# Retention by chunks with a carried state, and token-row jobs 512 columns wide in quarters of the depth

## The reference

```python
def retention_branch(p, cos, sin):            # S = 512, 4 heads, q and k 64 wide, v 128 wide
    q, k, v, g = jnp.split(p, ...)
    q = rotary(q, cos, sin); k = rotary(k, cos, sin) * (RET_QK_DIM ** -0.5)
    # chunks of 128 tokens, a decay gamma_h for each head
    scores = jnp.einsum('bhnid,bhnjd->bhnij', qc, kc) * decay_in[:, None]   # inside a chunk, j <= i
    inner = jnp.einsum('bhnij,bhnje->bhnie', scores, vc)
    kv = jnp.einsum('bhnjd,bhnje,hj->nbhde', kc, vc, k_dec)                 # what a chunk adds to the state
    R = R * chunk_decay + kv_n                                              # carried over the chunks
    cross = jnp.einsum('bhnid,nbhde,hi->bhnie', qc, R_prev, q_dec)
    y = inner + cross
    y = y * lax.rsqrt(jnp.mean(y * y, axis=-1, keepdims=True) + EPS)
    return y * jax.nn.silu(g)
```

## Time and profile before

| | |
|---|---|
| three runs | 2812.18, 2813.51, 2815.59 us; median 2813.51 |
| profiled execution | span 2810.8 us, 46630 instructions; the page gives no time of its own beside the span |
| TensorE | busy 2760.1 us, 98%, 18980 records |
| VectorE, ScalarE, GpSimd | 46%, 39%, 50% |
| granted TensorE clock | mean 0.997 |
| DMA | 413.98 MB, mean 147 GB/s |
| first stage, layer one | jobs 4 to 17: 41.95 to 143.67 us |
| first stage, layer two | jobs 4 to 17: 956.52 to 1059.04 us |

### The profile page before, as it was taken

How to read it: one execution, slowest core, us unless ns; L and a number is a source line. 1 busy time by engine, 2 the same in 40 slices (tenths; PEclk the granted TensorE clock), 3 DMA queues, 4 the chain that set the end, 5 groups by cost and what they waited for, 6 DMA issues and landing times. The chain is left out here.

```text
span 2810.8 us, 46630 instructions
## 1 busy us (share of the span) xinstructions
PE 2760.1 (98%) x18980; PEld 2059.2 (73%) x18981; DVE 1286.0 (46%) x1791; ACT 1101.1 (39%) x1618; POOL 1399.4 (50%) x1767
## 2 busy tenths in 40 slices
PE   8999999999999999999999999999999999999997
PEld 6777778888888877777788888877778764445543
DVE  6255433467751524543446775168855232222223
ACT  5485334343332448533434333355574321111112
POOL 6377446666665637744666665665655321111110
PEclk9999999999999999999999999999999999999999
DMA  5222122222232422212222223232222149999995
GB/s 182 74 87 73 48 106 91 85 93 103 91 112 98 163 75 87 72 49 105 91 86 91 105 90 113 93 113 81 93 91 94 63 190 407 419 415 411 414 409 232
DMA packets 63368, 413.98 MB, mean 147 GB/s; under 512 B 9792, under 2 KB 10560, under 8 KB 25920
## 3 DMA queue, kind: packets, MB, share of 16 engines
q1 hardware_dynamic: 63168, 411.18, 38.6%
HBM read 401.71 MB, written 4.19 MB: 144 GB/s over the span
## 5 line engine op out<-in xcount | busy, mean ns | idle before, releaser
L113 POOL TENSOR_TENSOR w_lo<-w,next_hi 128x256 fp32r<-128x256 f32 (+1 forms) x1272 | 1001.5, 820 | 623.4 <-ACT next_hi L1686 290.1
L1686 ACT CAST next_hi<-w 128x1024 fp32r<-128x1024 f32 (+1 forms) x152 | 156.9, 1032 | 462.4 <-PE bank L1504 443.0
L113 POOL TENSOR_TENSOR mid_w_lo<-w,mid_w_hi 128x256 fp32r<-128x256 f32 x240 | 198.6, 859 | 138.8 <-ACT mid_w_hi L2812 138.4
L3574 PE MATMUL bank<-moe_w,moe_hg 128*64 128x512 f32 x1024 | 225.8, 594 | 0.0
L3574 PEld LDWEIGHTS bank<-moe_w,moe_hg 128*64 128x64 f32 x1024 | 73.4, 137 | 141.1 <-issue 141.1
L3511 POOL COPY moe_quad_place<-moe_place 128x16 f32 (+1 forms) x7 | 1.4, 196 | 346.5 <-PE bank L3628 346.5
L1499 PE MATMUL bank<-h_hi,next_hi 128*128 128x512 f32 x688 | 170.8, 390 | 0.0
L1504 PE MATMUL bank<-h_hi,w_lo 128*128 128x512 f32 x688 | 169.9, 389 | 0.0
L1501 PE MATMUL bank<-h_lo,next_hi 128*128 128x512 f32 x688 | 169.9, 389 | 0.0
L1332 ACT CAST next_hi<-w 128x1024 fp32r<-128x1024 f32 x96 | 80.2, 835 | 206.6 <-PE bank L1530 151.6
L1499 PEld LDWEIGHTS bank<-h_hi,next_hi 128*128 128x128 f32 x688 | 129.1, 188 | 27.7 <-issue 1.0
(11 more groups left out here) (633 smaller groups left out, 6243.3 us busy)
## 6 DMA issues: line engine op xcount, KB each, us to landing
moe_w<-in_moe_w SPq DMA_DIRECT2D x128, 1024.0 KB, 13.1
moe_w<-in_moe_w SPq DMA_DIRECT2D x32, 2048.0 KB, 12.4
w<-in_ffn_up SPq DMA_DIRECT2D x44, 1024.0 KB, 4.8
w<-in_w_merge SPq DMA_DIRECT2D x48, 768.0 KB, 4.3
w<-in_w_in SPq DMA_DIRECT2D x30, 1024.0 KB, 4.8
w<-in_w_mid SPq DMA_DIRECT2D x29, 1024.0 KB, 4.8
w<-in_ffn_down SPq DMA_DIRECT2D x16, 1408.0 KB, 5.8
w<-in_w_out SPq DMA_DIRECT2D x16, 512.0 KB, 4.3
```

What stands on the lines that cost most here:

```text
L113: ins = nc.gpsimd.tensor_tensor(out[:, ks, :], raw[:, ks, :], high[:, ks, :].bitcast(F32), ALU.subtract)
L1686: nc.scalar.copy(split(B.w_hi, n), raw(n)).then_inc(f["w_hi"], 1)
L3574: mm = nc.tensor.matmul(bank[half_of(u), :], hg[:, k, slots_of(b, u)], w[:, u, k * 512:k * 512 + 512], start=(k == 0), stop=(k == KD - 1))
```

## The change

Retention follows the reference's chunks. The decay table holds 128 columns a head instead of 512, and a new table `qdec` (2 x 128 columns) holds the decay of the queries. VectorE multiplies the queries of chunks 1 to 3 with it (`decay_queries`). Behind job 8 TensorE transposes the keys of chunks 0 to 2 (`turn_keys`, 6 transposes into banks 6 and 7) and makes the scores inside the chunks of all four heads (`scores`, 16 matmuls of 64 rows and 128 columns, alternating between the two row halves, banks 2 to 5). VectorE writes the keys with their decay (`take_keys`) and the decayed scores (`decays`, one operation a head). Behind job 9 come the states that the chunks add (`chunk_states`, 12 matmuls of 128 rows with 64 columns stationary, alternating between the column halves); VectorE carries them on (`states`). Behind jobs 10 and 11 `values(t)` adds for two heads the products inside the chunks (8 matmuls of 128x128) and with the states (6 of 64 rows, alternating), into bank 2 + h. `squares` comes behind jobs 11 to 14; on ScalarE `square` in jobs 10 to 13 and `root` in jobs 11 to 14, root ahead of square.

A pair of token chunks is 512 columns in four quarters of the depth. A token job is a quarter: 4 token tiles x 3 products x 2 steps = 24 matmuls of 512 columns, a bank for each token tile, in the order 2, 3, 0, 1. ScalarE takes the tiles in the fourth quarter, three while it runs and one after it. The weights are laid out for it outside of the kernel. The first quarter of jobs 14 to 17 waits for `ret_done` of 2, as banks 2 and 3 are those of heads 0 and 1.

```diff
-        self.vt, self.decay = at(spare, 0, "vt", 4, S), at(y_rw, 0, "decay", RET_HEADS, S)
+        self.vt, self.decay = at(spare, 0, "vt", 4, S), at(y_rw, 0, "decay", RET_HEADS, P)
+        self.ktok, self.kv = at(y_rw, 2, "ktok", 2, 3, P), at(y_rw, 5, "kv", 2, 3, P)
+        self.qdec, self.qd = at(bonus, 4, "qdec", 2, P), at(spare, 8, "qd", 2, S)
...
+            sync.dma_start(B.qdec[:, :, :], T.dram["ret_qdec"]).then_inc(f["ret_loaded"], 16)
...
-                for m in range(4):
-                    bank = T.ps[m // 2][:, (m % 2) * 256:(m % 2) * 256 + 256]
-                    if t == 0 and m % 2 == 0:
-                        pe.wait_ge(f["took"][m // 2], c)
+                if quarter == 0 and i >= 2:
+                    pe.wait_ge(f["ret_done"], 2)
+                for m in TOKEN_TILES:
+                    if quarter == 0 and m < 2:
+                        pe.wait_ge(f["took"][m], c)
                     for lhs, w in ((h_hi, hi), (h_lo, hi), (h_hi, lo)):
-                        for k in range(half):
-                            if w is lo and m == 0:
-                                pe.wait_ge(f["w_lo"], pieces_until(n, k, half))
+                        for k in range(2):
+                            if w is lo and m == TOKEN_TILES[0]:
+                                pe.wait_ge(f["w_lo"], pieces_until(n, 2 * k + 1, half))
+                            mm = nc.tensor.matmul(T.ps[m][:, :], lhs(2 * quarter + k)[:, m * P:m * P + P], w[:, k, :], ...)
...
+            def scores():
+                pe.wait_ge(f["rotated"], 4)
+                for t in range(2):
+                    for c in range(4):
+                        now = slice(c * P, c * P + P)
+                        for u in range(2):
+                            q = slice(64 * u, 64 * u + 64)
+                            mm = nc.tensor.matmul(T.ps[2 + 2 * t + u][:, now], qk[q, 2 + t, now], qk[q, t, now],
+                                                  start=True, stop=True)
+                    mm.then_inc(f["ret_products"], 1)
+            def turn_keys():
+                        mm = nc.tensor.transpose(T.ps[6 + t][:, c * P:c * P + P], qk[:, 2 + t, c * P:c * P + P],
+                                                 T.ident[:, :])
+            def chunk_states():
+                            mm = nc.tensor.matmul(T.ps[6 + t][64 * u:64 * u + 64, c * P:c * P + P],
+                                                  B.ktok[:, t, c, 64 * u:64 * u + 64], vt[:, c, h * P:h * P + P],
+                                                  start=True, stop=True)
+            def values(t):
+                pe.wait_ge(f["ret_decayed"], SCORES_DECAYED + 2 * t + 2)
+                for c in range(4):
+                    for u in range(2):
+                        nc.tensor.matmul(T.ps[2 + h][:, c * P:c * P + P], vt[:, c, h * P:h * P + P],
+                                         B.sc[:, h, c * P:c * P + P], start=(c == 0), stop=False, ...)
+                pe.wait_ge(f["kv_ready"], t + 1)
+                for c in range(1, 4):
+                    for u in range(2):
+                        mm = nc.tensor.matmul(T.ps[2 + 2 * t + u][:, c * P:c * P + P], B.kv[q, t, c - 1, :],
+                                              B.qd[q, t, c * P:c * P + P], start=False, stop=(c == 3), ...)
...
-                if n in (10, 12, 14, 16):
-                    squares((n - 10) // 2)
-                if n in (8, 10, 12, 14):
-                    scores((n - 8) // 2)
-                if n in (9, 11, 13, 15):
-                    values((n - 9) // 2)
+                if n == 8:
+                    turn_keys()
+                    scores()
+                if n == 9:
+                    chunk_states()
+                if n in (10, 11):
+                    values(n - 10)
+                if n in (11, 12, 13, 14):
+                    squares(n - 11)
...
-                if n in (9, 11, 13, 15):
-                    square((n - 9) // 2)
-                if n in (10, 12, 14, 16):
-                    root((n - 10) // 2)
+                if n in (11, 12, 13, 14):
+                    root(n - 11)
+                if n in (10, 11, 12, 13):
+                    square(n - 10)
...
+            def states(t):
+                dve.wait_ge(f["ret_products"], STATES_SUMMED + t + 1)
+                link(nc.vector.tensor_copy(B.kv[:, t, 0, :], T.ps[6 + t][:, 0:P]))
+                for c in range(1, 3):
+                    ins = nc.vector.scalar_tensor_tensor(out=B.kv[:, t, c, :], in0=B.kv[:, t, c - 1, :],
+                                                         scalar=B.qdec[:, t, P - 1:P],
+                                                         in1=T.ps[6 + t][:, c * P:c * P + P], op0=ALU.mult, op1=ALU.add)
```

More of the change, by code:

```diff
@@ L225 @@
 TOKEN_CHUNKS = (2, 3, 7, 8)
+TOKEN_TILES = (2, 3, 0, 1)
 RW_FIRST, U_FIRST = 18, 30
@@ L413, in feature_job @@
                 mm.then_inc(f["done"], 1)
-            def scores(h):
-                q = slice(64 * (h % 2), 64 * (h % 2) + 64)
+            def scores():
                 pe.wait_ge(f["rotated"], 4)
-                for jc in range(4):
-                    if h:
-                        pe.wait_ge(f["decayed"], 4 * (h - 1) + jc + 1)
-                    nc.tensor.matmul(T.ps[2 + jc][:, 0:S - jc * P], qk[q, 2 + h // 2, jc * P:jc * P + P],
-                                     qk[q, h // 2, jc * P:S], start=True, stop=True).then_inc(f["scored"], 1)
@@ L425, in values @@
-            def values(h):
-                if h == 0:
-                    for t in range(2):
-                        pe.wait_ge(f["took"][t], 4)
-                else:
-                    pe.wait_ge(f["ret_done"], h)
-                for jc in range(4):
-                    pe.wait_ge(f["decayed"], 4 * h + jc + 1)
-                    mm = nc.tensor.matmul(T.ps[6][:, jc * P:S], vt[:, jc, h * P:h * P + P],
-                                          B.sc[:, jc, 0:S - jc * P], start=(jc == 0), stop=(jc == 3),
-                                          skip_group_check=True)
-                mm.then_inc(f["summed"], 1)
+                for t in range(2):
[6 more added lines that the diff above has]
+                    mm.then_inc(f["ret_products"], 1)
@@ L861, in _ @@
                 rotate(t)
+            dve.wait_ge(f["rotated"], 4)
+            for t in range(2):
+                decay_queries(t)
+            for t in range(2):
+                take_keys(t)
             for h in range(RET_HEADS):
                 decays(h)
-                if h == 3:
-                    shift(12, 12, B.sg_tmp[:, 0, :])
-                    shift(13, 13, B.sg_tmp[:, 1, :])
+            for t in range(2):
+                states(t)
+            for h in range(RET_HEADS):
+                if h >= 2:
+                    shift(10 + h, 10 + h, B.sg_tmp[:, h - 2, :])
                 head_out(h)
@@ L3999, in layout @@
     w_in = weight_chunks(np.concatenate([a["w_in"][:, :, cols], a["w_in"][:, :, len(cols):]], axis=-1), 256)
+    for n in range(0, len(TOKEN_CHUNKS), 2):
+        both = [FRONT_ORDER[c] for c in TOKEN_CHUNKS[n:n + 2]]
+        columns = w_in[:, both].reshape(L, 2, P, 2, KD // 2, 256)
+        w_in[:, both] = columns.transpose(0, 3, 2, 4, 1, 5).reshape(L, 2, P, -1)
     out["w_in"] = w_in[:, :FRONT_CHUNKS]
```

116 lines of the change are left out of this document (77 added, 39 removed).

## The result

The changed kernel took 2791.61 us (median of 4 runs, 2789.2 to 2796.58), the kernel before 2813.78 (2812.18 to 2815.59) beside it: ratio 0.9924, 95% interval 0.9909 to 0.9938. The forecast was 2790.0. Five more runs later gave 2798.84 (2789.96 to 2799.42), ratio 0.9939, interval 0.9926 to 0.9953. All nine together have a median of 2792.4, but they lie in two heaps, five at 2789.2 to 2792.4 and four at 2796.6 to 2799.4, while the kernel before, run beside them, kept to 2811.7 to 2816.5 (over all its 39 runs on record, 38 lie at 2811.7 to 2817.4 and one at 2821.5). So there are two questions: whether the 23.5 us of the sum are there, and what takes back some 7 us in some executions.

A forecast was written before the change was run, and what follows sets the result against it. TensorE, busy 98% of the span, was taken as the bound. Terms 5.1 + 17.4 + 1.1 - 0.5 + 0.45 = 23.5 us, taken from 2813.5, gave 2790.0 us (chance 0.73), range 2785.5 to 2800.

The forecast's parts named there:

- Token jobs: 16 token jobs over two layers: 24 matmuls of 512 columns take 5.44 us a job instead of 5.76; 5.1 us gained.
- Retention: TensorE's work behind jobs 8 to 11: 9.9 us a layer instead of 18.6, matmuls pairing on two halves; 17.4 us gained.
- Job 18: TensorE's 0.55 us wait for a tile of `v` at the start of job 18 goes; 1.1 us gained for two layers.
- ScalarE's loop: Root and square in each of jobs 11 to 14: 6.3 us against TensorE's 6.4, 0.1 to spare; 0.5 us charged.
- Low half at job 6: Cast and POOL's four pieces for a pair's first quarter: 5.7 us against 6.6, so hidden, 0.9 to spare.
- Weight of job 6 in layer two: 640 KB less ahead of it in the queue, landing 1.6 to 1.9 us sooner, wait about 0.1; 0.45 us gained.
- Stages: The two stages, one in each layer, were to be shorter by some 11.6 and 12 us, all else as before.
- The stages behind move forward as a block.: Stages after the changed ones start by TensorE's progress and TensorE is full there too, so the whole gain reaches the span.
- rival 4: Stage ends earlier but the last stage's expert-weight streaming takes the time back; no change, 2812 us; chance 0.03.
- rival 1: Retention matmuls on the two halves don't pair at 128 columns, costing 8.9 us; 2798.9 us; chance 0.12.

The follow-up runs named there:

- tokens_narrow: Changed kernel with each 512-column matmul of the token jobs made as two of 256 columns; 2799.69 us.
- one_half: Changed kernel with scores, cross products and chunk states of both heads on the same array half, so nothing can pair (output wrong); 2804.47 us.
- tables_late: Changed kernel with masks, centre and mixing tables fetched behind the weights of chunks 3 and 4 instead of ahead of them; 2796.54 us.
- late_and_shift: Changed kernel with masks, centre and mixing tables fetched behind later weights, plus 64 extra satisfied waits on TensorE in layer two; 2788.5 us.
- changed_again: The changed kernel itself, unedited, in five more runs; 2798.84 us, the profiled execution 2789.96 us.
- rows_in_turn: Changed kernel with scores and cross products made all on one row half, then all on the other, instead of alternating; 2798.54 us.
- square_twice: Changed kernel with ScalarE computing each of the four squares a second time into an unread tile; 2797.74 us (two runs).
- tables_heavy: Changed kernel with two tables loaded a second time at the head of the stage, 640 KB more, read by nobody; 2795.87 us (two runs).
- cols_in_turn: Changed kernel with the chunk states made all on one column half, then all on the other, instead of alternating; 2797.55 us.

## Why the prediction was right, and where it wasn't

- **Token jobs, 5.1 us.** Jobs 4 to 7 measure 22.03 us, less 0.15 of a wait at job 6 (the 0.77 at 53.40 us where others are 0.62): 5.47 a job for 5.44. tokens_narrow gives 4.4 us for both layers. Right.
- **Retention, 17.4 us.** Behind jobs 8 to 11 stand 2.75, 1.7, 2.9 and 2.9 us, 10.3 for 9.9, so 16.7 us gained for 17.4. The mechanism, pairs on two halves, is shown by one_half (8.7 us). The size was off by 6 ns a record: 62 and not 56, and by the going in and out, 0.4 us for 0.3. The 81 ns at 128 columns that was quoted from the Trainium skill ("TensorE: Matmul & The Clock Gate", Back-to-back issue gap) is no floor for records on alternating halves.
- **Job 18, 1.1 us.** Gone in both layers.
- **ScalarE's loop, -0.5 us.** It idles 0.4 to 0.5 us a round, 0.1 had been reckoned, and TensorE never waits for it. The 0.5 us that was charged for nothing makes up most of the 0.7 by which retention fell short: the sum came out close partly by luck. Job 14 starts at 109.27 us and its token tile's release (VectorE's second head) ends at 109.12: 0.15 to spare for the 0.2 predicted.
- **Low half at job 6, "0.9 to spare".** Wrong. In layer one the fourth piece is 0.15 us late even with the cast on time; POOL's pieces are slower there than half of its eight.
- **Weight of job 6 in layer two, 0.45 us.** That fewer bytes ahead bring it forward is shown by tables_late and late_and_shift. The size was too good: the cast came 1.2 us sooner against job 4 (8.20 to 7.02), for 1.6 to 1.9, and the wait stayed at 0.6 us in this execution, and was nil in changed_again (cast at 6.51). With the same bytes three edited kernels had it at 8.6 to 10.1 and waited 1.76 us, more than the 1.65 that the prediction had for a weight that comes no sooner. So in the profiles the term runs from a gain of 0.5 us to a loss of 1.2 and the reduced clock behind it.
- **Stages.** 11.2 and 11.3 us shorter in the first profile, 11.2 and 12.0 in changed_again, for 11.6 and 12.
- **"The stages behind move forward as a block."** That held in the two profiled executions to within 1.2 us, and by their times in five of nine. The other four are some 7 us longer (2796.6 to 2799.4 for 2789.2 to 2792.4). The likeliest value was right; the mean of the nine, 2794.3, lies 4 us above it. What fails, at least in the kernels with one edit more, is the assumption that outside the stage only data and engines can be late. The refill of TensorE's own instructions is a transfer too, and the edits moved it against the merge transfers. No rival named it; rival 4 had asked for a transfer that doesn't start by TensorE's progress, and this one does, but by the count of its instructions. Whether the changed kernel's four long executions have this stall, the late weight of job 6 or the reduced clock of the last stage wasn't seen, since the two that were profiled took 2791.25 and 2789.96 us. Why the kernel before doesn't spread so (in its one profile the recurrence has no such gap above 0.6 us) is argued from where its refills fall, not tried.
- **What the time alone would have said.** The later five runs have a median of 2798.84 us, which is the 2798.9 of rival 1, though the halves do pair. Only the rows of the stage tell the two apart.

## What to carry to other kernels

Put small matmuls of two heads on the two halves of the array in alternation, and keep them together: each going in and out costs as much as six of their records. If a kernel that got shorter spreads over two values, look in the trace for a gap of the bounding engine with no releaser, and then at the instruction queue under it. Look also at the wait for a weight behind a full queue, which differed by 1.8 us between profiles here. A few harmless instructions, or a large transfer moved, can be worth more than the next edit.

## What the runs showed of the hardware

- Records of 128 columns: 111 ns alone, 115 to 117 when all are on one half, 62 in alternation. A sequence of one half overlaps with the sequence of the other half behind it (rows_in_turn: 86 ns a record on average).
- TensorE's instructions come in packets of 16 KB, on average one for 267 records (matmuls and weight loads). That they are TensorE's is read from their coming at nearly the same record numbers of it in each execution. One that fell behind a transfer of 768 KB waited for its end, and TensorE started again 2.4 us after that packet's start (1236.77 to 1239.14). In tables_late it ran dry 178 records behind the place of the undisturbed refill. The Trainium skill ("Runtime: NRT & Kernel Launch", Instruction fetch mechanics) has the cost of crossing such a block mostly hidden; the measurement decides otherwise where a large transfer is ahead of it.
- Behind such a gap the granted clock was 0.50, 1.2 GHz, for 6.8 us in tables_late and square_twice, for 3.4 us in tables_heavy, cols_in_turn and one_half, and not at all in tokens_narrow. So 3.1 us of idle time put tables_late back by 6.1 us against changed_again, and 2.9 put tokens_narrow back by 3.2.
